# Three token groups of 128, 176 and 256 columns in place of two, in a decoder layer with expert gathering

## What is computed

```
qry = (xi @ w_query).reshape(block, 8 heads, 2, 128);  s = qry . sub_keys      # 128 scores in each half
top 16 of each half -> top 16 of the sums -> idx (16 experts per token and head), gate = softmax(top_s)
hid = gelu(xi . expert_u[idx]);   y = sum over heads and k of gate * hid * expert_v[idx]
```

## Time and profile before

| | before |
|---|---|
| median of three runs | 4440.15 us |
| the profiled execution, from first to last instruction | 4437.4 us |
| VectorE busy | 3281.7 us, 74% |
| TensorE busy (matmuls) | 2369.9 us, 53% |
| GpSimd busy | 2373.6 us, 53% |
| ScalarE busy | 587.6 us, 13% |
| moved by DMA | 1513.7 MB, 341 GB/s on average |
| of it by GpSimd's queue, the gathers among it | 1158.9 MB |

### The profile page before, as it was taken

How to read it: one execution, slowest core, us unless ns; L and a number is a source line. 1 busy time by engine, 2 the same in 40 slices (tenths; PEclk the granted TensorE clock), 3 DMA queues, 4 the chain that set the end, 5 groups by cost and what they waited for, 6 DMA issues and landing times. The chain is left out here.

```text
span 4437.4 us, 35313 instructions
## 1 busy us (share of the span) xinstructions
PE 2369.9 (53%) x11697; PEld 1879.6 (42%) x11697; DVE 3281.7 (74%) x4293; ACT 587.6 (13%) x1463; POOL 2373.6 (53%) x1345
## 2 busy tenths in 40 slices
PE   6999999988589999989749774100000000000000
PEld 5888888777466666666537553000000000000000
DVE  2333333305789999989876888999998899999998
ACT  2222222301112222222210011000000000000000
POOL 1001001001445555555465544888887888888886
PEclk8999999999789999999959887555555555555555
DMA  6766666487789999999999964999999999999998
GB/s 174 223 206 208 195 195 200 138 307 236 267 341 407 406 412 413 409 379 401 368 371 411 398 248 170 397 422 422 420 422 389 413 422 422 421 417 419 407 418 352
DMA packets 444573, 1513.70 MB, mean 341 GB/s; under 512 B 42684, under 2 KB 276848, under 8 KB 278488
## 3 DMA queue, kind: packets, MB, share of 16 engines
q0 software_dynamic: 161840, 1158.85, 64.4%
q1 hardware_dynamic: 269880, 251.94, 17.7%
q10 hardware_dynamic: 12672, 100.67, 5.7%
HBM read 1384.96 MB, written 126.21 MB: 341 GB/s over the span
## 5 line engine op out<-in xcount | busy, mean ns | idle before, releaser
L1962 DVE SCALAR_TENSOR_TENSOR ex_y<-ex_ring,ex_wt,ex_y 128x2048 f32<-128x2048 f32 x538 | 1272.2, 2365 | 102.2 <-DMA ex_ring<-in_peer_v_dram,idx_all 47.3
L1947 DVE CUSTOM_DVE_ANT_0 ex_ring<-ex_ring,ex_xi 128x2048 f32<-128x2048 f32 x544 | 1244.3, 2290 | 125.0 <-DMA ex_ring<-in_peer_u_dram,ex_idx_s 49.9
L1869 POOL DMA_INDIRECT ex_ring<-in_peer_u_dram,idx_all x384 | 791.2, 2060 | 310.8 <-DVE ex_hid L1947 207.0
L1869 POOL DMA_INDIRECT ex_ring<-in_peer_v_dram,idx_all x384 | 762.8, 1986 | 240.5 <-issue 118.3
L1901 PE MATMUL ex_fold<-ex_y,const 128*32 128x512 f32 (+1 forms) x48 | 24.9, 682 | 1113.2 <-DVE ex_y L1962 1113.2
L870 PE MATMUL heads_b_pj<-xnT_b,lead 128*128 128x304 f32 x2048 | 601.3, 431 | 15.2 <-DVE mixT_b L1539 9.4
L1901 PEld LDWEIGHTS ex_fold<-ex_y,const 128*32 128x32 f32 (+1 forms) x48 | 6.3, 137 | 1131.3 <-DVE ex_y L1962 1114.5
L1869 POOL DMA_INDIRECT ex_ring<-in_peer_u_dram,ex_idx_s x160 | 317.8, 1986 | 206.9 <-DVE ex_hid L1947 154.7
L870 PEld LDWEIGHTS heads_b_pj<-xnT_b,lead 128*128 128x128 f32 x2048 | 373.9, 195 | 126.5 <-issue 15.2
L1869 POOL DMA_INDIRECT ex_ring<-in_peer_v_dram,ex_idx_s x160 | 289.3, 1808 | 199.6 <-DVE ex_y L1962 133.1
L870 PE MATMUL heads_a_pj<-xnT_a,heads_a_w 128*128 128x256 f32 x1216 | 316.2, 398 | 1.8 <-DMA heads_a_w<-in_w_in_dram 1.8
(11 more groups left out here) (590 smaller groups left out, 4036.9 us busy)
## 6 DMA issues: line engine op xcount, KB each, us to landing
lead<-w_scratch SPq DMA_DIRECT2D x64, 1024.0 KB
heads_a_w<-in_w_in_dram SPq DMA_DIRECT2D x38, 1024.0 KB, 6.2
w_scratch<-heads_a_w ACTq DMA_DIRECT2D x38, 1024.0 KB, 4.2
lead<-in_w_in_dram SPq DMA_DIRECT2D x26, 1024.0 KB, 5.7
w_scratch<-lead ACTq DMA_DIRECT2D x26, 1024.0 KB, 4.1
out_a_w<-in_w_out_dram SPq DMA_DIRECT2D x7, 2048.0 KB, 14.4
w_out_scratch<-out_a_w ACTq DMA_DIRECT2D x7, 2048.0 KB, 9.4
out_b_w<-w_out_scratch SPq DMA_DIRECT2D x7, 2048.0 KB, 12.8
```

The source lines that it names most:

```text
L1869: pool.indirect_dma_start(self.ring[:, i % RING, :], None, self.tables[which], bass.IndirectOffsetOnAxis(ap=self.index(s, g, k), axis=0)). ...
L1947: nc.vector.tensor_tensor_reduce(ring, ring, self.tokens(s)[:], 1.0, 0.0, ALU.mult, ALU.add, self.hid[:, g % 2, k:k + 1]).then_inc(self.se ...
L1962: nc.vector.scalar_tensor_tensor(y, ring, wt, y, ALU.mult, ALU.add).then_inc(self.sem["consumed"], 1)
```

## The change

There are three groups: FIRST of one tile of 128 columns, MIDDLE of 176 columns (tiles of 128 and 48) and LAST of 256 columns (two tiles). The stages run three times. The items have new quotas: 192 items of 6 groups in the stages of MIDDLE, 384 items of 12 groups in those of LAST, and the other 16 groups, 512 items, in `rest_of_experts`. MIDDLE reads w_in from the scratch and keeps keys, values, state and the last raw columns for LAST, as FIRST does; LAST reads the scratch too. w_out and the query weights have no scratch any more and are read from the inputs in every group, the query weights in pieces of 256 columns, and `mix_out` has two accumulators per tile. The token buffer and the sum of the items exist twice and alternate from set to set (`side`), so a set waits for the set before the last. Sums are no longer folded on TensorE and copied on ScalarE; each part of a set is added to the output by a DMA of its own, parts of the same tokens at least 6 items apart.

```diff
-FIRST = Group("a", 0, (0, 128, 256), 0)
-LATER = Group("b", 256, (0, 128, 256, 304), 2)
+FIRST = Group("a", 0, (0, 128), 0)
+MIDDLE = Group("b", 128, (0, 128, 176), 1)
+LAST = Group("c", 304, (0, 128, 256), 3)
+GROUPS = (FIRST, MIDDLE, LAST)
...
-        front(nc, ins, outs, mem, scr, LATER, stream, OVERLAP)
-        rest_of_experts(nc, stream)
+        front(nc, ins, outs, mem, scr, MIDDLE, OVER_FIRST)
+        front(nc, ins, outs, mem, scr, LAST, OVER_MIDDLE)
+        rest_of_experts(nc, mem["stream"])
...
-OVERLAP = {"norm": 14, "heads": 330, "out": 48, "ffn": 8, "route": 36}
+OVER_FIRST = {"norm": 14, "heads": 124, "out": 30, "ffn": 8, "route": 16}
+OVER_MIDDLE = {"norm": 14, "heads": 290, "out": 40, "ffn": 8, "route": 32}
...
-        for group, parts, groups, folds in (
-            (FIRST, [prompt_part(0, FIRST, 1)], HEADS, 1),
-            (FIRST, [split(r, FIRST, 0, slice(T0, T0 + half)) for r in range(2)], HEADS // 2, 1),
+        for group, parts, groups in (
+            (FIRST, [split(r, FIRST, 0, slice(T0, T0 + half)) for r in range(2)], HEADS // 2),
             (FIRST, [self.Part(r * NS, FIRST, 0, slice(0, NS), r * HEADS // fold, y_sample) for r in range(fold)],
-             HEADS // fold, fold),
-            (LATER, [prompt_part(0, LATER, 0)], HEADS, 1),
-            (LATER, [split(r, *p) for r in range(2) for p in ((FIRST, 0, slice(T0 + half, P)), (LATER, 2, slice(0, LATER.rows[2])))],
-             HEADS // 2, 2),
-            (LATER, [prompt_part(0, LATER, 1)], HEADS, 1),
+             HEADS // fold),
+            (MIDDLE, [prompt_part(0, MIDDLE, 0)], HEADS),
+            (MIDDLE, [split(r, *p) for r in range(2) for p in ((FIRST, 0, slice(T0 + half, P)),
+                                                               (MIDDLE, 1, slice(0, MIDDLE.rows[1])))], HEADS // 2),
+            (LAST, [prompt_part(0, LAST, 0)], HEADS),
+            (LAST, [prompt_part(0, LAST, 1)], HEADS),
         ):
...
     def before(self, s):
 
-        return next((r for r in reversed(self.sets[:self.sets.index(s)]) if r.second == s.second), None)
+        at = self.sets.index(s)
+        return self.sets[at - 2] if at >= 2 else None
...
+    def sum_out(self, pool, s, part):
+
+        pool.wait_ge(self.sem["consumed"], self.last_v(s) + 1)
+        if self.y_outs:
+            pool.wait_ge(self.sem["y_out"], 16 * self.y_outs)
         alone(pool, self.sem["admitted"])
...
-                sp.dma_start(w[:, c % 2], w_out[:, :, c * GW:(c + 1) * GW] if group.samples else scr["w_out"][c]
-                             ).then_inc(sem[f"w_in{c % 2}"], 16)
+                sp.dma_start(w[:, c % 2], w_out[:, :, c * GW:(c + 1) * GW]).then_inc(sem[f"w_in{c % 2}"], 16)
...
-                    if c >= 1:
-                        pe.wait_ge(sem["group_added"], (c - 1) * group.n + i + 1)
+                    if c >= 2:
+                        pe.wait_ge(sem["group_added"], (c - 2) * group.n + i + 1)
```

More of the change, by code:

```diff
@@ L240, in build @@
-        rest_of_experts(nc, stream)
[L243 to L249, removed]
-        with ExitStack() as rows:
-            mem["gain"] = rows.enter_context(nc.sbuf_tensor(f"gain_{group.tag}", [P, D], F32))
-            mem["hres"] = rows.enter_context(nc.sbuf_tensor(f"hres_{group.tag}", [P, group.n, D], F32))
-            mix_out(nc, ins, mem, scr, group, stream, quotas["out"])
-            mem["xiT"] = mem["mixT"]
-            ffn_norm(nc, ins, outs, mem, scr, group, stream, quotas["ffn"])
-        route(nc, ins, mem, scr, group, stream, quotas["route"])
+        keep(ctx, "packed", [P, KT * WIDEST])
@@ L381, in _ @@
             if stream:
-                stream.spread(sp, FIRST)
+                stream.spread(sp, GROUPS[GROUPS.index(group) - 1])
             else:
@@ L599, in heads @@
     KS = 2 * P + NS
-    keys = KA if samples else KW
+    keys = EDGES[group.slot + T]
+    before, rowed = EDGES[group.slot], samples or group.last
     blocks = [(EDGES[i], EDGES[i + 1]) for i in range(group.slot + T)]
@@ L604, in heads @@
     PAGE_SETS = 4
+    STORES = [o for o in (whole_rows(group), rest_rows(group)) if o]
     lead = mem["lead"]
@@ L710, in state_out @@
     def state_out(h, t):
-        if samples and t == T - 1:
+        if not group.last and t == T - 1:
             return mem["S_kept"][:, h, :]
@@ L1520, in gdn @@
                             dve.wait_ge(sem["S_ready"], h * T + t)
-                        if t == T - 1 and not samples and h > 0:
+                        if t == T - 1 and group.last and h > 0:
                             dve.wait_ge(sem["gp_out"], 16 * h)
@@ L1769, in __init__, with known_after, sums_due @@
         self.taken = self.issued = self.activated = self.y_outs = self.xi_ins = 0
+    def known_after(self, group):
+        return 2 * TOPK * self.cuts[GROUPS.index(group) + 1]
+    def sums_due(self):
+        due = {}
+        for s in self.sets:
+            for r, part in enumerate(s.parts):
+                turn = sum(part.slot == other.slot for other in s.parts[:r])
+                due.setdefault(min(self.last_v(s) + RING * (1 + turn), self.items - 1), []).append((s, part))
+        return due
     def run(self, g):
-        return (0, self.cut) if g < self.cut else (self.cut, self.groups - self.cut)
+        first = max(c for c in self.cuts if c <= g)
+        return first, min(c for c in self.cuts if c > g) - first
     def turn_first(self, first, groups, turn):
@@ L1846, in spread_all @@
     def spread_all(self, group):
-        return sum(64 if part.folded else 32 for s in self.sets if not s.whole and (s.group is FIRST or s.group is group)
-                   for part in s.parts)
+        earlier = GROUPS[:GROUPS.index(group) + 1]
+        return sum(64 if part.folded else 32 for s in self.sets if not s.whole and s.group in earlier for part in s.parts)
     def gather(self, pool, taken):
@@ L1855, in gather @@
             s = self.set_of[g]
-            if which == 0 and g == s.first and k == 0 and g > 0 and self.u_item(g - 1, TOPK - 1) >= taken:
+            if which == 0 and g == s.first and k == 0 and self.before(s) and self.u_item(self.before(s).end - 1, TOPK - 1) >= taken:
                 break
@@ L1953, in take @@
                     earlier = self.before(s)
[L1954 to L1957 removed]
+                    if earlier:
+                        dve.wait_ge(self.sem["y_out"], 16 * sum(len(r.parts) for r in self.sets[:self.sets.index(earlier) + 1]))
                     nc.vector.tensor_scalar(y, ring, wt, None, ALU.mult).then_inc(self.sem["consumed"], 1)
```

324 lines of the change are left out of this document (151 added, 173 removed).

## The result

The changed kernel takes **4681.6 us** (median of 4 runs, 4669.2 to 4692.4) against 4437.3 beside it: 1.0549 [1.0529, 1.0569] times as long, 5.5% slower. Forecast were 4632 us and a range of 4440 to 4790. The profiled execution has a span of 4681.0 us.

The account below looks back on a forecast made before the run. TensorE was taken to bound the kernel until 1178 us, with nothing gathered, and mostly DMA afterwards. Groups a, b, c and the end sum to 805 + 1077 + 1447 + 1300 = 4629 us of span, forecast 4632; range 4440 to 4790.

Parts of the forecast that it names:

- The mechanism: Whole kernel: start 373 us earlier, end stage 366 shorter, 931 us added between by the third pass; 4% slower.
- clock rival: Middle heads: TensorE's clock granted at only 0.6, its work 100 us a head, total 4808 us; chance 9%.
- rival without coupling: Heads stages run at their fullest resource, 64, 62 and 107 us a head; total 4428 us; chance 16%.
- First heads: Group a's heads at 128 columns: TensorE work 57 us, 69 us a head with standstill, stage 585 against 838.
- Middle heads: Group b's heads, 176 columns, 124 items: 78 us a head, bounds 62 and 88; heads stage 681 us.
- term of 18 us for coupling and table loads: Middle heads: 18 us a head lost to items holding chain steps back on VectorE, the convolution, head's end and table loads.
- Out b and c: Output stages of middle and last group: 143 and 168 us, from items, 50 us of directly read weights and other loads.
- Trainium skill's rule: Direct reads: fixed overhead per packet, some 9% at 1 KB; reads 39 us, not 50, total about 20 us lower.
- Norms of b and c: Norm stages of middle and last group: 60 us, waiting for a spread index before its first item, and 56 us.
- The rest: Last stretch after all stages: 512 items at 2.555 us, 1308, less 8, so 1300 us.
- 8 us taken off for the second pair of item buffers: Last stretch: alternating buffers let the next set's first gathers start before the old tokens are free, 1308 to 1300 us.
- a POOL wait on them finds them landed: Last stretch: added output parts stand at least a ring of 6 items apart, so waiting on them costs nothing.

Follow-up runs that it names:

- no-item head: Middle head of the changed kernel with 0 instead of 124 items in the middle group's heads, these done after all stages: 4890.5 us.
- eight lengths listed above: Stage times of the eight first heads: 565 to 594 us in kernels with this code unchanged, 563 in the changed kernel with head weights read directly in all groups.
- seven kernels of this code: Three-group kernels with the same first-heads code, the changed kernel and variants of it; eight first heads took 565 to 594 us, TensorE standing 66 to 70.
- packed: Changed kernel with output and query weights written to scratch by the first group and read there by b and c: 4623.6 us, 1.0431.
- eight items left: Changed kernel with the middle group's routing quota 8 instead of 16, so 8 known items remain at the later two borders: 4666.0 us, 1.0529.

## Why the prediction came out as it did

**The mechanism held.** The start comes 344 us earlier (373 forecast), the rest is 334 us shorter (366), and the added stages between take more than both. The clock rival fell: 0.97 and 0.91 in the heads of b and c, and near 1.2 GHz (0.50 to 0.62) only in ffn, the norms and tails of b and c, and the rest. The rival without coupling fell too: a middle head is 73.2 us, not 62 to 64, and the no-item head alone is 65.4. The total was 50 us low. The last group's heads are right within 18 us, both later routings within 11.

**First heads, 69 forecast, 72.4 measured; stage 620 for 585.** Their DMA work of 62 to 63 us and the chain stalls were in the sum; TensorE's own work was not 57 but 64 us, 511 in eight heads. About half of these 7 us is a matter of counting: the sum took 93.4 us for a head before, the same view has it busy 96.9 (678.61 in seven), as each busy stretch ends with a pipeline's end. For the other half, the step that failed is that the granted clock of heads a before, 0.94, was taken to stay. In 36 us windows, two to a head, it alternates:

```profile
224.00:260.00 36.00, 31.21 (x266) 29.74 (x265) 17.19 (x75) 17.66 (x41) 5.92 (x8) 1.00 1.02 328
260.00:296.00 36.00, 34.51 (x227) 31.59 (x227) 5.96 (x21) 4.21 (x15) 2.83 (x2) 0.81 0.80 242
```

At 0.81 the 34.5 busy us hold 227 matmul records, at 1.00 the 31.2 hold 266; of the projection alone a record takes 0.182 and 0.140 us of busy time (15.5 us for 85, 24.0 for 172), where the forecast had 0.111. The eight lengths listed above go from 563 to 594 us as the clock goes from 0.91 to 0.86, about 6 us for each 0.01. As the standstill is the same in all seven kernels of this code, the difference is in the matmuls' own length. What made the clock differ between kernels is open.

**Middle heads, 78 forecast, 73.2 measured.** The term of 18 us for coupling and table loads was too large: TensorE's work is 64.7 us, not 60, and what is added to it 8.5. The row used for it shows the delay of one item at one hop, 0.7 to 0.9 us; on average an item's hold costs 0.25 and its transfer another 0.25. That most items meet no waiting hop is the likely reason. The tail, 44 for 52, erred to the same side.

**Out b and c, 143 and 168 forecast, 163 and 182 measured.** I had counted 14 us a stage for direct reads (50 for 36), from an estimated speed of reads with nothing beside them, 278 GB/s. Beside gathers they cost 46 and 45. The other terms, 129 and 154 without that, were 12 and 17 us too high, and covered part of it: packed, the stages are 117 and 137 us to the last addition, with TensorE busy 115 and DMA at 1.01 of the time. The Trainium skill's rule, which would have taken 11 us off each, pointed further away.

**Norms of b and c, 60 and 56 forecast, 76 and 70 measured.** 5 us of each difference are the border: the forecast ends a norm that long before the first projection and counts it in the heads (880 + 5), the measured stages don't. Norm c's other 9 us are the empty ring: 12 are gone with eight items left. Norm b starts with an empty ring of necessity, as nothing is known before; its seven items between two tiles are the likely cause of the other 11 us, which was read from the trace and not tested.

**The rest, 1300 forecast, 1332 measured.** The 8 us taken off for the second pair of item buffers were a guess that no run bears out; they do nothing at the first border, where the ring is dry, and with eight items left the stretch is still 10 us over 2.555 an item. The clause "a POOL wait on them finds them landed; if it doesn't, up to 12 us for each of eight" was wrong at the last border, 13.0 us, once. So of the 32 us, 8 are the guess, 14 the empty ring and that wait, and 10 are not placed.

## What to carry to other kernels

Add up DMA busy and idle time on both sides of a cut before splitting work to start a bound resource earlier: the idle time saved at the start must not come back in stages that have too little known work to fill it, and each further pass over the weights is DMA work added, to be paid where DMA is the bound. Price small-run reads where they will stand, beside the traffic that they share engines with, and ask what stops when they come late; in lockstep loops a late load silences the queue as well. Where a source of overlapped work is given quotas, leave a few pieces over at each border, so that the next stage doesn't start on an empty ring.

## What was not expected of the hardware

- Small runs beside gathers: 2 MB in 1 KB runs landed in 24.0 us, in long runs in 12.7; 1 MB in 512-byte runs took 17.3 us to land in the last group's heads, and a head 136 us instead of 108.
- Accumulating writes: an addition of at most 384 KB to the output, queued behind six gathers, held its issuer for 13.0 us.
- The same eight heads of the same code took 565 to 594 us between kernels, at granted clocks of 0.91 to 0.86; the runs of one three-group kernel spread over 13 to 40 us, where those of the kernel before stay within 14.
